# Moving a quarter of the first expert's down-projection and the final norm's weights into buffers that are free earlier, and reloading whole places of the weight ring

## The reference

```
xn = RMSNorm(h); proj = xn @ w_in          # 9744 columns
mixed = sig(g_a)*(o_a @ w_proj_a) + sig(g_b)*(o_b @ w_proj_b)   # attention and gated linear attention
h = h + mixed @ w_out
h = h + MoE(RMSNorm(h))                    # top 4 of 32 experts
  hu  = x @ w_up[e] + b_up[e]              # w_up[e]   1024 x 2048, 8 MB
  act = min(glu,7) * sig(1.702 glu) * (clip(lin,-7,7) + 1)
  y   = act @ w_down[e] + b_down[e]        # w_down[e] 1024 x 1024, 4 MB
output = RMSNorm(h) * lnf_w
```

## Time and profile before

| | |
|---|---|
| median of 3 runs | 1247.16 us (1246.35 to 1247.44) |
| profiled execution | 1249.05 us, span 1247.3 us |
| TensorE busy | 1162.8 us (93%) |
| VectorE / ScalarE busy | 392.8 / 241.5 us |
| bytes moved | 456.95 MB, mean 366 GB/s |
| loads of 4 MB in the expert stage, issue to landing | 31.1 us median |
| clock of TensorE | 1.00 up to 480 us, mean 0.981 |

### The profile page before, as it was taken

The page is one execution under the profiler, slowest core; times in us unless marked ns, Lnnn a source line. Parts: engine busy times, 40 slices in busy tenths (PEclk is TensorE's granted clock), DMA queues, the critical chain, the costliest instruction groups (busy, mean ns, idle before and its releaser), DMA issues.

```text
span 1247.3 us, 16249 instructions
## 1 busy us (share of the span) xinstructions
PE 1162.8 (93%) x6984; PEld 593.3 (48%) x6984; DVE 392.8 (31%) x670; ACT 241.5 (19%) x334; POOL 10.8 (1%) x29
## 2 busy tenths in 40 slices
PE   9999999999999998989898988898998989989997
PEld 8888887888643343333333333333333333333332
DVE  7865746666522121111211111111121112111112
ACT  5333445554410010000100000000010001000002
POOL 2000000000000000000000000000000000000000
PEclk9999999999999999999999999999999999999999
DMA  8745333377999999999999999999999999999996
GB/s 264 262 157 186 136 135 135 135 276 283 369 415 431 432 427 436 428 429 436 430 430 436 430 429 436 431 429 435 432 429 434 433 429 433 435 428 431 426 427 262
DMA packets 45997, 456.95 MB, mean 366 GB/s; under 512 B 5540, under 2 KB 5688, under 8 KB 30952
## 3 DMA queue, kind: packets, MB, share of 16 engines
q1 hardware_dynamic: 45512, 455.09, 87.6%
q10 hardware_dynamic: 448, 1.32, 0.3%
HBM read 455.35 MB, written 1.05 MB: 366 GB/s over the span
## 4 chain that ended last, share of the span: by engine, by line
PE 55%; DMA 38%; DVE 4%; ACT 1%; issue 1%; SPq 0%; DVEq 0%
PE ps L1400 54%; DMA ring<-in_w_up_dram 27%; DMA arena<-in_w_up_dram 7%; DMA ring<-in_w_down_dram 3%; DMA ring<-in_w_in_dram 1%; DVE w_split L900 1%; PE ps L1909 1%; ACT w_split L614 0%; PE ps L1594 0%; PE ps L1805 0%; DVE arena L945 0%; DVE arena L949 0%; DVE arena L1101 0%; DVE arena L1067 0%; PE ps L1702 0%
## 5 line engine op out<-in xcount | busy, mean ns | idle before, releaser
L1400 PE MATMUL ps<-ring,arena 128*64 128x512 f32 x2304 | 523.8, 608 | 53.1 <-DMA ring<-in_w_up_dram 51.7
L1400 PEld LDWEIGHTS ps<-ring,arena 128*64 128x64 f32 x2304 | 163.6, 140 | 382.5 <-issue 301.4
L1400 PE MATMUL ps<-arena 128*64 128x512 f32 (+3 forms) x920 | 202.5, 563 | 19.0 <-DMA arena<-in_w_up_dram 17.5
L1319 DVE TENSOR_SCALAR arena<-ps 128x512 f32<-128x512 f32 x32 | 22.1, 692 | 490.0 <-PE ps L1400 490.0
L1400 PEld LDWEIGHTS ps<-arena 128*64 128x64 f32 (+1 forms) x920 | 77.9, 148 | 131.5 <-issue 100.5
L900 DVE TENSOR_TENSOR w_split<-ring,w_split 128x2048 fp32r<-128x2048 f32 x48 | 109.9, 2291 | 81.9 <-ACT w_split L614 81.6
L810 ACT ACTIVATE arena<-arena 128x512 f32<-128x512 f32 x32 | 20.2, 631 | 554.9 <-DVE arena L1319 554.9
L1400 PE MATMUL ps<-w_split,x_split 128*128 128x512 f32 x528 | 123.5, 392 | 0.7 <-ACT arena L650 0.5
L614 ACT ACTIVATE w_split<-ring 128x2048 fp32r<-128x2048 f32 x47 | 89.7, 1914 | 112.0 <-PE ps L1400 96.1
L1400 PEld LDWEIGHTS ps<-w_split,x_split 128*128 128x128 f32 x528 | 98.4, 188 | 21.6 <-issue 1.2
L1400 PE MATMUL ps<-x_split,w_split 128*128 128x256 f32 (+1 forms) x544 | 93.1, 331 | 1.1 <-DVE arena L1115 1.0
(11 more groups left out here) (245 smaller groups left out, 603.1 us busy)
## 6 DMA issues: line engine op xcount, KB each, us to landing
ring<-in_w_up_dram SPq DMA_DIRECT2D x40, 4096.0 KB, 31.1
ring<-in_w_down_dram SPq DMA_DIRECT2D x21, 4096.0 KB, 29.9
arena<-in_w_up_dram SPq DMA_DIRECT2D x14, 4096.0 KB, 31.1
ring<-in_w_in_dram SPq DMA_DIRECT2D x17, 2048.0 KB, 7.8
arena<-in_w_down_dram SPq DMA_DIRECT2D x7, 4096.0 KB, 30.0
ring<-in_w_up_dram SPq DMA_DIRECT2D x12, 2048.0 KB, 23.0
arena<-in_w_up_dram SPq DMA_DIRECT2D x4, 2048.0 KB, 21.5
ring<-in_w_up_dram SPq DMA_DIRECT2D x8, 1024.0 KB, 8.7
```

Source lines behind the costliest of these rows:

```text
L1319: dve.tensor_scalar(glu_c, ps[bank][:, :], LIMIT, None, ALU.min).then_inc(glu_ok, 1)
L1400: return pe.matmul(dst, lhsT, rhs, start=start, stop=stop, skip_group_check=True)
```

## The change

The old names `xres`, `load_up_half`, `half_signals` and `halves_landed` go. The masks, `gla_w`, `causal` and `glr_w` are put into one tile `shared` of 1088 columns, and `lnf` is laid over it. `second_half` is a new 1 MB place in the arena, at `G0 - HALF`, where `y_split` and `act_last` lie later; `sel_g` is moved out of it.

```diff
+        second_half = at(G0 - HALF, HALF)
-        sel_g = moe(2 * TT * CAP).rearrange(...)
+        sel_g = at(M0 + 1920, 2 * TT * CAP).rearrange(...)
+        shared = sb("shared", [P, 1088])
+        lnf = shared[:, 0:D]
-        lnf = at(M0, 1024)
-        first_down_at = ((half_place, place_half(0, 0)), (place_half(0, 1), place_half(1, 0)))
+        first_down_at = ((place_half(0, 0), place_half(0, 1)), (half_place, second_half))
```

SyncE, in the dense stage (the loads of chunks 21 and 22) and behind it:

```diff
                 if c == C_PB + 1:
                     load_first(sp, 0)
                     load_first(sp, 1)
+                    sp.wait_ge(sig_ok, 3)
+                    sp.dma_start(lnf, lnf_w....broadcast_to([P, D])).then_inc(lnf_in, 16)
                 if c == C_WO:
                     sp.wait_ge(proj_done, PROJ_UNITS)
                     load_up(sp, 1, 0, 4)
+                    sp.wait_ge(proj_done, U_PB)
+                    load_down_half(sp, 0, 1, 1, first_down_at[1][1], second_half_in)
...
             sp.wait_ge(lg_ps, 2)
+            load_down_half(sp, 0, 1, 0, first_down_at[1][0], early_in[1])
+            sp.wait_ge(half_used, 1)
             load_down_half(sp, 0, 0, 0, first_down_at[0][0], early_in[0])
-            sp.wait_ge(half_used, 1)
+            sp.wait_ge(chunk_used, 1)
             load_down_half(sp, 0, 0, 1, first_down_at[0][1], chunk_in[0])
-            sp.wait_ge(chunk_used, 1)
-            load_down_half(sp, 0, 1, 0, first_down_at[1][0], early_in[1])
-            sp.wait_ge(half_used, 2)
-            load_down_half(sp, 0, 1, 1, first_down_at[1][1], chunk_in[1])
+            sp.wait_ge(chunk_used, 2)
+            load_up(sp, 3, 1, 1)
             for c in range(UP_CHUNKS):
-                sp.wait_ge(half_used, 3 + c)
-                load_up_half(sp, 2, c, 0, ...)
                 sp.wait_ge(chunk_used, 3 + c)
-                load_up_half(sp, 2, c, 1, ...)
+                load_up(sp, 2, c, 2 + c)
             down_chunks(1, 0, 3 * UP_CHUNKS + DOWN_CHUNKS)
-            sp.wait_ge(chunk_used, 2 * UP_CHUNKS + DOWN_CHUNKS)
-            one_turn(0, 0, UNROLL, 2)
+            sp.wait_ge(chunk_used, 2 * UP_CHUNKS + 1)
+            load_up(sp, 3, 0, 0)
+            sp.wait_ge(chunk_used, 3 * UP_CHUNKS)
+            load_up_pair(sp, 3, 1, 3 * PER_EXPERT)
+            down_chunks(2, 0, 3 * PER_EXPERT + DOWN_CHUNKS)
+            one_turn(0, 0, UNROLL, UNROLL - 1)
```

ScalarE no longer issues the load of `lnf`, and VectorE writes the residual pieces over `xs2`:

```diff
-                act.activation(xs2p[:, 1, t, :], xres[t], ACT.Copy).then_inc(mid_ok, 1)
-            for t in range(TT):
-                act.wait_ge(low_ok[t], 1)
-            act.dma_start(lnf, ...).then_inc(lnf_in, 16)
+                act.activation(xs2p[:, 1, t, :], xs2[:, t, :], ACT.Copy).then_inc(mid_ok, 1)
-                dve.tensor_tensor(xres[t], xs2[:, t, :], xs2p[:, 0, t, :], ALU.subtract)
+                dve.tensor_tensor(xs2[:, t, :], xs2[:, t, :], xs2p[:, 0, t, :], ALU.subtract)
```

More of the change, by code:

```diff
@@ L144, in layer @@
         xs2 = at(TMP0, 2048).rearrange("p (t c) -> p t c", t=TT)
-        xres = [at(TMP0 + 2048, D), at(M0, D)]
         place = [3072]
@@ L151, in moe @@
             return at(place[0] - count, count)
+        second_half = at(G0 - HALF, HALF)
         xin = moe(1024).rearrange("p (b k s) -> p b k s", b=2, k=KT)
         glu_c, sig_c, lin_c, act_c, actT = (moe(512) for _ in range(5))
-        sel_g = moe(2 * TT * CAP).rearrange("p (t s) -> p t s", t=TT)
+        sel_g = at(M0 + 1920, 2 * TT * CAP).rearrange("p (t s) -> p t s", t=TT)
         def moe_r(name, shape, count):
@@ L170, in layer @@
         selT_f = at(M0 + 1664, SEQ)
-        masks = sb("masks", [P, NG, 384], BF16)
+        shared = sb("shared", [P, 1088])
+        masks = shared[:, 0:576].bitcast(BF16).rearrange("p (g c) -> p g c", g=NG)
+        gla_w = shared[:, 576:576 + DV]
+        causal = shared[:, 832:832 + P].bitcast(I32)
+        glr_w = shared[:, 960:960 + P].rearrange("p (k r) -> p k r", k=KT)
+        lnf = shared[:, 0:D]
         ident = sb("ident", [P, P])
@@ L175, in layer @@
         ones = sb("ones", [P, P], BF16)
-        causal = sb("causal", [P, P], I32)
         slot_no = sb("slot_no", [P, P])
@@ L182, in layer @@
         ln2P0 = sb("ln2P0", [P, KT])
-        glr_w = sb("glr_w", [P, KT, RANK])
         glrT = sb("glrT", [RANK, SEQ])
@@ L229, in layer @@
         early_in = [sem(f"early_in{i}") for i in range(6)]
-        ln2P_in = sem("ln2P_in")
+        ln2P_in, second_half_in = sem("ln2P_in"), sem("second_half_in")
         x_in = [sem(f"x_in{t}") for t in range(TT)]
@@ L377, in load_down_part @@
             sp.dma_start(chunk_at[n % PLACES].rearrange("p (s n) -> p s n", s=4), rows).then_inc(chunk_in[n % PLACES], 16)
-        LATE_DOWN = {1: 32, 2: 48}
+        AHEAD = 2 * PLACES + 1
+        LATE_UP, LATE_DOWN = {1: 16, 2: 32}, {1: 32, 2: 48}
         half_place = xnT[:, :, :].rearrange("p k t -> p (k t)")
@@ L393, in load_down_half @@
             sp.dma_start(dst.rearrange("p (s n) -> p s n", s=2), rows[:, 2 * half:2 * half + 2, :]).then_inc(landed, 16)
-        def load_up_half(sp, e, c, half, dst, landed):
-            rows = w_up[0, e, c // 2 * 512:c // 2 * 512 + 512, :].rearrange("(p s) n -> p s n", s=4)
-            sp.dma_start(dst, rows[:, 2 * (c % 2) + half, :]).then_inc(landed, 16)
         def late_in(u, c):
@@ L447, in _ @@
                     load_first(sp, 1)
+                    sp.wait_ge(sig_ok, 3)
+                    sp.dma_start(lnf, lnf_w.rearrange("(a n) -> a n", a=1).broadcast_to([P, D])).then_inc(lnf_in, 16)
                 if c == C_WO:
@@ L791, in _ @@
                 act.wait_ge(res_ok[t], 1)
-                act.activation(xs2p[:, 1, t, :], xres[t], ACT.Copy).then_inc(mid_ok, 1)
-            for t in range(TT):
-                act.wait_ge(low_ok[t], 1)
-            act.dma_start(lnf, lnf_w.rearrange("(a n) -> a n", a=1).broadcast_to([P, D])).then_inc(lnf_in, 16)
+                act.activation(xs2p[:, 1, t, :], xs2[:, t, :], ACT.Copy).then_inc(mid_ok, 1)
             act.wait_ge(turns_ok, 1)
@@ L1288, in _ @@
                 dve.wait_ge(hi_ok, t + 1)
-                dve.tensor_tensor(xres[t], xs2[:, t, :], xs2p[:, 0, t, :], ALU.subtract).then_inc(res_ok[t], 1)
+                dve.tensor_tensor(xs2[:, t, :], xs2[:, t, :], xs2p[:, 0, t, :], ALU.subtract).then_inc(res_ok[t], 1)
             for t in range(TT):
                 dve.wait_ge(mid_ok, t + 1)
-                dve.tensor_tensor(xs2p[:, 2, t, :], xres[t], xs2p[:, 1, t, :], ALU.subtract).then_inc(low_ok[t], 1)
+                dve.tensor_tensor(xs2p[:, 2, t, :], xs2[:, t, :], xs2p[:, 1, t, :], ALU.subtract).then_inc(low_ok[t], 1)
             dve.wait_ge(lg_exp, 1)
@@ L1835, in first_up @@
                         pe.wait_ge(xin_ok, 1)
-                    up_part(0, 0, c, c, 0, FIRST_BANK, False).then_inc(half_used, 1)
+                    ins = up_part(0, 0, c, c, 0, FIRST_BANK, False)
+                    if c == 0:
+                        ins.then_inc(half_used, 1)
                     if c == 0:
@@ L1844, in first_up, with up @@
                         gather()
-            def up(i, m, first, half_signals=0, halves_landed=False, between=None, by_chunk=False, late=None):
+            def up(i, m, first, between=None, by_chunk=False, ahead=False, late=None):
                 up_bias(m)
                 for c in range(UP_CHUNKS):
-                    if by_chunk or c % 2 == 0:
+                    if ahead and first + c == AHEAD:
+                        pe.wait_ge(chunk_in[1], 32)
+                    elif by_chunk or c % 2 == 0:
                         chunk_landed(i, first + c)
                     if late is not None and c % 2:
[L1854 to L1859, removed]
+                        pe.wait_ge(late_in(late, c), LATE_UP[late])
+                    up_part(i, m, first + c, c, 0, (0, 1), False)
                     up_part(i, m, first + c, c, 1, (0, 1), c == UP_CHUNKS - 1).then_inc(chunk_used, 1)
@@ L1869, in first_down @@
                     pe.wait_ge(early_in[d], 16)
-                    chunk_landed(0, 2 * UP_CHUNKS + d)
+                    if d == 0:
+                        chunk_landed(0, 2 * UP_CHUNKS)
+                    else:
+                        pe.wait_ge(second_half_in, 16)
                     for k in range(4):
@@ L1891, in down @@
                         if last and k == 0:
-                            pe.wait_ge(early_in[2 + d], 32)
+                            pe.wait_ge(early_in[2 + d], 16)
                         if last and k == 2 and d == 0:
@@ L1925, in last_share, with expert_pe @@
                         ins.then_inc(sum_ps, 1)
-            def expert_pe(i, u, first=False, halves_landed=False, late=None, starts=False, keeps=False):
+            def expert_pe(i, u, first=False, by_chunk=False, ahead=False, late=None, starts=False, keeps=False):
                 def at_n(k):
@@ L1941, in expert_pe @@
                 if first:
-                    up(i, u + 1, up_end(u) - UP_CHUNKS, half_signals=2, between=first_between, by_chunk=True)
```

(5 more changed lines are left out.)

3 lines of the change are left out of this document (removed).

## The result

The changed kernel takes 1249.28 us (median of 22 runs, 1246.41 to 1250.82) against 1247.06 us before: a ratio of 1.0017, 95% interval 1.0011 to 1.0023. It is 2.2 us slower, by less than the 0.2% that I had set as the bound, but outside the range of the prediction, and on the other side of zero. A second set of 11 runs on another occasion gave 1249.00, ratio 1.0015 (1.0006 to 1.0024). The profiled execution took 1249.90 us, span 1248.1.

A forecast was written before the change was run, and what follows sets the result against it. The unbroken stream of weights plus a 12.7 us tail was taken to bound the kernel. A stream gain of 4.3 less a 2.6 us stall gave 1.7 to 2.3, taken as 2.0: 1245.2 us, range 1242.2 to 1248.0.

The forecast's parts named there:

- The bound: Whole kernel: the end is when the stream of weights ends plus 12.7 us; before 340 us TensorE's delay costs one for one.
- (1): A down-projection quarter, issued at 277 to 280 us, leaves the unbroken stream: 2.4 us gained, up to 2.7.
- (2): lnf leaves the stream, where it landed at 340 to 346 us: 1.2 to 2.4 us gained, taken as 1.7.
- (3): Place 1 reloaded at once, in 2 MB pieces: a hole of 0.7 us and a gain of 0 to 1.5, taken as cancelling.
- (4): Room for expert 3's second 4 MB, at 381.3 us, caps the stream's gain at 4.4 us, or about 4.9.
- (5): Dense stage: new loads ahead of chunks 22 and 23 stop TensorE near 304 us for 2.6 us (2.0 to 3.5).
- B: Rival: the dense-stage stall halves TensorE's clock, 1.7 us more, leaving no gain; 1247.0 us, chance 0.14.
- D: Rival: full queue holds SyncE, chunk 23 issued late, TensorE stands 5.3 us; 2.6 slower, 1249.8 us, chance 0.08.
- A: Rival: the dense stage doesn't stall, or under 1 us; gain 4.4 to 4.9, 1242.5 us, chance 0.22.
- C: Rival: loads leave the stream but nothing comes out, its 2.6 us gain equal to the stall; 1247.2 us, chance 0.11.

The follow-up runs named there:

- e9: e5 plus ten useless matmuls (about 2.1 us) ahead of TensorE's unit 45; 1245.59 us, ratio 0.9993.
- e5: Changed kernel with lnf and the quarter behind expert 0's third chunk, expert 3's second 4 MB cut in two, first piece a chunk earlier; 1243.33 us.
- e5_again: The same kernel as e5, run once more; 1243.37 us, ratio 0.9973.
- e1: Changed kernel with only the quarter of the first down-projection issued later, behind expert 0's third chunk; 1246.61 us, ratio 0.9994.
- e1_again: The same kernel as e1, run once more; 1245.32 us, ratio 0.9983.
- e7: e2 without the early reload of place 1, expert 3's first 4 MB coming as one pair as before the change; 1247.64 us, ratio 1.0006.
- e4: Changed kernel with expert 3's second 4 MB cut in two 2 MB pieces, the first issued one chunk earlier; 1246.53 us, ratio 0.9997.
- e10: e2 with expert 3's second 4 MB cut in two 2 MB pieces, both issued at the old moment; 1245.98 us, ratio 0.9995.
- e4_again: The same kernel as e4, run once more; 1246.30 us, ratio 0.9989.
- e2: Changed kernel with the quarter and then lnf both issued later, behind expert 0's third chunk; 1245.40 us, ratio 0.9982.
- e2_again: The same kernel as e2, run once more; 1245.07 us, ratio 0.9984.
- e3: Changed kernel with ten useless matmuls (about 2.1 us) where TensorE stops, ahead of unit 45; 1248.44 us, ratio 1.0012.
- e8: e4 with the ten useless matmuls of e3 ahead of unit 45; 1246.05 us, ratio 0.9990.
- e6: e5 with lnf loaded by ScalarE behind the residual pieces, as before the change; 1244.10 us, ratio 0.9976.

## Why the prediction was wrong

*The bound.* Right: the end is the stream's end plus a tail, and a delay of TensorE ahead of the stream costs one for one (e9).

*(1) and (2), what leaves the stream.* Right in size. With the stop and the hole gone the kernel is 3.9 and 3.8 us faster (e5 and e5_again); by the landings 4.5 to 4.9. The parts had 4.1; the sum went on with 4.3, which is more than its own parts give. In the dense stage lnf delays chunk 22 by 1.4 us (1.7), and the quarter delays chunk 23 by 2.4 more (2.5): it lands in 14.0 and 14.1 us with lnf alone ahead (e1, e1_again), in 16.5 with both.

*(3), the early reload.* Wrong in what it is. I wrote that it can only help where the queue would run dry, and cancelled it. e7 shows where it would: with two loads gone the stream moves 55 GB/s from 346 to 350 us, and without the reload 2.2 us or more are lost.

*(4), the cap: the step that failed.* I had seen that expert 3's second 4 MB would meet a nearly empty queue, and priced that with a 2 MB load issued to an empty queue (2.8 us beside its data), part of which a queue that is not quite empty would cover. At this place it takes 4.7: 9.7 us of data took 14.4 in the changed kernel, and the 2.3 us of queue did not bring it down to the 12.5 of an empty one. The cap was 16.9 - 14.4 = 2.5 us and not 4.4; at the next load the gain against TensorE is 19.8 - 17.7 = 2.1. e4 and e5 show it by issuing earlier (landing 14.9 to 15.4, 2.7 and 2.1 us of time), e10 that the size of the pieces is not the reason.

*(5), the stop.* Right: chunk 23 3.9 us later (4.2), `w_high(46)` released by it, `mix_low(1)` last, a stop of 2.33 us (2.6). With the hole closed such a stop costs 2.9 to 3.2 us (e4 and e4_again against e5), of which its length is 2.4 to 2.5 (the delays) and the rest can be the half clock, see B. Against the changed kernel e2 and e2_again gain 3.6 to 4.2; what this is more stays unexplained.

*The rivals.* B, the half clock, had 0.14, and both profiled executions of the changed kernel show it: 107.18 - 102.96 = 4.2 us of delay, 2.3 of stop and 1.9 of slow matmuls; B had 2.6 + 1.7. Over many executions it averages 0.2 to 0.8 (e3, e8, e4_again against e9). It was right in mechanism where it comes, in about a third of the executions, and it met a smaller cap; I had given each rival its own row and not their product. D's place was right and its mechanism wrong: SyncE was held longer at expert 1's first chunk than before (4.50 us against 2.32 in the earlier trace rows), but chunk 23 still went out at its time, 284.6, and the order alone counted. That D's 1249.8 us come nearest to the measured 1249.28 is luck. The issue in question:

```profile
274.07 4.50 SPq L367 DMA_DIRECT2D ring<-in_w_up_dram  x1
```

A and C are out: the stop came, and the loads do save the stream some 4 us (3.8 by the medians, 4.5 to 4.9 by the landings).

*The sum again.* With the cap at 2.1 to 2.5 instead of 4.3 and the stop at 2.3, the forecast of 2.0 faster becomes 0.2 slower to 0.2 faster, and with 0.2 to 0.8 for the half clock 0 to 1.0 slower. From the medians alone it is 0.8 to 1.5 slower: 3.8 gained with neither loss (e5), 1.7 to 2.1 for the hole (e2 against e5), 2.9 to 3.2 for the stop (e4 against e5). Measured were 2.2 and 1.9. The cap and the half clock thus take the forecast past zero, and the last 0.4 to 1.4 us have no cause that a run shows; the intervals are wide enough to hold most of them.

*What stays open.* Why a load at 381 us needs 4.7 us beside its data and one at 308.7 us 2.8; where the last 0.4 to 1.4 us of the slowdown come from; why the first set of e1 was wide; and what drops the clock near 328 us in executions without a stop.

## What to carry to other kernels

When a kernel ends with an unbroken stream of loads, ask of each edit two things apart: how late it makes the engine that frees the buffers, and how much it leaves queued at the first load that meets a thin queue. The gain is capped at that load, and what counts is the moment of its issue: issue it as soon as the first part of its room is free. A load that is moved ahead of the stream pays only if nothing that is needed soon stands behind it in the queue; here issuing both loads some 20 us later, behind all of the dense stage's chunks, was enough to turn 2 us slower into 1.7 to 2.1 us faster (e2, e2_again). With the first piece of the pair issued a chunk earlier as well it became 3.8 to 3.9 us faster (e5, e5_again), the fastest version that was run.

## What the runs showed of the hardware that was not expected

- A load issued 2.3 us before the load ahead of it had landed (e10, 2 MB; the changed kernel, 4 MB) still left a hole of 2.5 us; issued 5.8 us before (e5_again) it left none.
- TensorE's granted clock fell to 0.50 at 330 to 334 us in the profiled executions of two kernels without a wait of over 0.5 us in front of it (e6, e7), where it is busy with short matmuls of the router and the first gather, and stayed at 1.00 in the others. Against e5 that cost 4.2 us of delay, more than twice what the drop behind the stop cost (1.9 us).
- Behind stops of nearly the same length the clock fell (2.33 and 2.5 us, the changed kernel) or stayed (2.16 us in e4, 2.2 in e4_again). In the changed kernel's trace it fell only after TensorE had restarted at 306.1 us: 1.00 in 305 to 306, 0.87 in 306 to 307, 0.50 in 307 to 310, and 1.00 again from 311 us on.
